# One-hot products of the dense tokens' weights: from float32 to bfloat16 pieces

## The reference, cut to what matters

```
idx = i_half * N_KEYS + i_half'            # 16 of 128 x 128 for each head
g = softmax(top_s)
h = gelu(einsum('td,thkd->thk', xb, u[idx]))
out = einsum('thk,thkd->td', g * h, v[idx])
```

## Time and profile before

| | us |
|---|---|
| median of three runs (1388.97 to 1390.58) | 1390.19 |
| the profiled execution's own time | 1392.18 |
| its span in the trace | 1390.4 |
| mean granted TensorE clock | 0.999 |

### The profile page before, as it was taken

One profiled execution on the slowest core, in us unless ns is written; L12 is line 12 of the kernel. 1 busy time (PEld: TensorE's weight loads), 2 busy tenths in 40 slices (PEclk: granted clock), 3 DMA queues, 4 the chain that ended last, 5 costly groups with the idle time before them and its releaser, 6 DMA issues.

```text
span 1390.4 us, 16195 instructions
## 1 busy us (share of the span) xinstructions
PE 1367.2 (98%) x5402; PEld 935.1 (67%) x5402; DVE 1056.4 (76%) x2365; ACT 438.4 (32%) x1219; POOL 599.5 (43%) x516
## 2 busy tenths in 40 slices
PE   7999999999999999999999999999999999999999
PEld 5656648567588888888899999995444444444443
DVE  4535445799899999998589899998768667766665
ACT  2533522444411111113677887882000000000000
POOL 0000001632855554442356655564667745544540
PEclk9999999999999999999999999999999999999999
DMA  8322334985999999996899999999999999999998
GB/s 308 138 108 111 121 125 183 362 314 196 403 389 411 409 352 374 342 350 234 299 377 407 385 398 395 389 382 402 388 410 409 410 409 409 409 409 409 410 409 311
DMA packets 121762, 467.68 MB, mean 336 GB/s; under 512 B 13776, under 2 KB 14160, under 8 KB 115152
## 3 DMA queue, kind: packets, MB, share of 16 engines
q0 software_dynamic: 73728, 268.47, 49.8%
q1 hardware_dynamic: 47664, 197.66, 36.8%
q10 hardware_dynamic: 288, 0.52, 0.1%
HBM read 462.67 MB, written 3.93 MB: 336 GB/s over the span
## 4 chain that ended last, share of the span: by engine, by line
PE 94%; DVE 3%; ACT 2%; issue 1%; DMA 0%; SPq 0%; ACTq 0%; DVEq 0%
PE BANKS L941 32%; PE BANKS L965 32%; PE BANKS L741 11%; PE BANKS L733 10%; PE BANKS L960 4%; PE BANKS L924 1%; PE BANKS L713 1%; PE BANKS L857 1%; PE BANKS L768 1%; PE BANKS L778 0%; DMA BIG<-w_in 0%; PE BANKS L829 0%; DVE NMX L1574 0%; ACT BIG L1122 0%; DVE UV L1638 0%
## 5 line engine op out<-in xcount | busy, mean ns | idle before, releaser
L1685 POOL DMA_INDIRECT UV<-u,IDX x152 | 174.1, 1145 | 398.8 <-DVE IDX L1513 261.2
L1685 POOL DMA_INDIRECT UV<-v,IDX x159 | 191.1, 1202 | 165.9 <-DVE UV L1638 91.3
L1643 DVE SCALAR_TENSOR_TENSOR X<-UV,HG,X 128x1024 f32<-128x1024 f32 x159 | 203.7, 1281 | 39.3 <-DMA UV<-v,IDX 37.1
L941 PE MATMUL BANKS<-T 128*128 128x256 f32 x1024 | 229.2, 379 | 0.0
L965 PE MATMUL BANKS<-T,BIG 128*128 128x512 f32 x512 | 225.2, 592 | 0.0
L965 PE MATMUL BANKS<-Y,BIG 128*128 128x512 f32 x512 | 225.1, 592 | 0.0
L941 PE MATMUL BANKS<-T,Y 128*128 128x256 f32 x992 | 221.9, 379 | 0.0
L1638 DVE SCALAR_TENSOR_TENSOR UV<-UV,Y 128x1024 f32<-128x1024 f32 x152 | 184.9, 1221 | 42.2 <-DMA UV<-u,IDX 40.8
L941 PEld LDWEIGHTS BANKS<-T 128*128 128x128 f32 x1024 | 192.0, 190 | 24.9 <-issue 0.2
L941 PEld LDWEIGHTS BANKS<-T,Y 128*128 128x128 f32 x992 | 186.0, 190 | 24.0
L965 PEld LDWEIGHTS BANKS<-Y,BIG 128*128 128x128 f32 x512 | 97.3, 190 | 122.5 <-issue 122.5
(11 more groups left out here) (258 smaller groups left out, 1222.2 us busy)
## 6 DMA issues: line engine op xcount, KB each, us to landing
T<-u_t SPq DMA_DIRECT2D x64, 512.0 KB
T<-v SPq DMA_DIRECT2D x64, 512.0 KB
Y<-v SPq DMA_DIRECT2D x64, 512.0 KB
Y<-u_t SPq DMA_DIRECT2D x62, 512.0 KB
BIG<-w_in SPq DMA_DIRECT2D x23, 1024.0 KB, 6.7
BIG<-w_q SPq DMA_DIRECT2D x16, 1024.0 KB, 7.4
BIG<-w_out SPq DMA_DIRECT2D x8, 1024.0 KB, 5.9
UV<-v,IDX POOLq DMA_INDIRECT x159
```

The source lines that it names most:

```text
L941: last = nc.tensor.matmul(PS[(i + 2) % 4][:, 0:HT], ub[:, c, :], T8[:, 1, c, :], start=(c == 0), stop=(c == KC - 1))
L1643: stt(xb, row, HG[:, n % 2, i % UNIT:i % UNIT + 1], xb, ALU.mult, ALU.add).then_inc(used, 1)
L1685: pool.indirect_dma_start(row_place(s), None, u if kind == "ru" else v, bass.IndirectOffsetOnAxis(IDX[:, b, c:c + 1], 0)).then_inc(row_in[ ...
```

## The change

The products of `og` are made in bfloat16. The one-hots are exact in it. The weight (float32, 24 bits of mantissa) is cut into three bfloat16 pieces of which the sum is the weight, so that each product becomes three that add up in PSUM: 12 products in a group in place of 4 float32 ones (which the trace counts as 8 MATMUL, two for each). A new step `sp` (`split_weights`) cuts the weights of a block, on DVE, straight from the PSUM bank of `sel`; the first two pieces lie in one 32-bit word (`WUPPER`), so that one scaled copy writes both. `oh` is now: DVE compares for j and for i, both in bfloat16, four tokens innermost; ACT scales the one-hot of j with `WUPPER` into `UPPER` (float32 words, read by PE as `HALVES`, every second bfloat16) and with `WLOWER` into `LOWER`. The bank is laid out token by token (t j) in place of (j t). ACT's part of `oh` waits for DVE's (`oh_j`), where before it waited for PE alone. `IOTAS`, a bfloat16 table of the key numbers, is written once. Small tables of the mixer (`DT`, `DTS` and others) become views of a new tile `STEPS`, which later holds the one-hot of j.

```diff
-    work += [first] + on("sel", 0) + rows(9) + on("oh", 0) + [second] + rows(3) + on("oh", 1) + [sums, keys, columns]
+    work += [first] + on("sel", 0) + rows(5) + on("sp", 0) + rows(4) + on("oh", 0) + [second] + rows(3) + on("oh", 1) + [sums, keys, columns]
...
+        if k == 2:
+            o += on("sp", 1)
...
+        KIJ = KT3[:, 0, :].bitcast(BF16).rearrange("p (a t) -> p a t", a=2)
+        WUPPER, WLOWER = KT3[:, 1, :], KT3[:, 2, :]
...
                 elif step == "og":
                     pe.wait_ge(oh_i, i + 1)
-                    pe.wait_ge(oh_ja, i + 1)
+                    pe.wait_ge(oh_w, i + 1)
                     if i in (0, 3):
-                        pe.wait_ge(selt_done, 4 if i else 2)
+                        pe.wait_ge(selt_done, 2 if i else 1)
+                        pe.wait_ge(split_done, 2 if i else 1)
...
-                    bank = PS[4 + i % 4][:, :].rearrange("p (j t) -> p j t", t=NTOK)
                     for k in range(NTOK):
-                        last = nc.tensor.matmul(bank[:, :, k], ONEHOT[:, i % 2, 0, k, :], ONEHOT[:, i % 2, 1, k, :],
-                                                start=True, stop=True)
+                        pieces = HALVES[:, i % 2, k, :, 1], HALVES[:, i % 2, k, :, 0], LOWER[:, i % 2, k, :]
+                        for m, piece in enumerate(pieces):
+                            last = nc.tensor.matmul(PS[4 + i % 4][:, k * P:(k + 1) * P], ONEHOT_I[:, i % 2, :, k], piece,
+                                                    start=(m == 0), stop=(m == 2))
...
                 elif step == "oh":
...
+                    act.wait_ge(oh_j, i + 1)
+                    for k in range(NTOK):
                         t = i * NTOK + k
-                        nc.scalar.activation(ONEHOT[:, i % 2, 1, k, :], IOTA, ACT.Abs, bias=KT3[:, 1, t:t + 1],
-                                             scale=-1.0).then_inc(oh_abs, 1)
...
+                        nc.scalar.activation(UPPER[:, i % 2, k, :], ONEHOT_J[:, i % 2, :, k], ACT.Copy,
+                                             scale=WUPPER[:, t:t + 1])
+                        last = nc.scalar.activation(LOWER[:, i % 2, k, :], ONEHOT_J[:, i % 2, :, k], ACT.Copy,
+                                                    scale=WLOWER[:, t:t + 1])
+                    last.then_inc(oh_w, 1)
...
+            def split_weights(i):
+                dve.wait_ge(selt_done, i + 1)
+                if i == 0:
+                    nc.vector.tensor_copy(IOTAS, bc(IOTA, 2, NTOK))
...
             def onehots(g):
...
+                tt(ONEHOT_J[:, g % 2, :, :], IOTAS, bc(KIJ[:, 1, part], 1, NKEY), ALU.is_equal).then_inc(oh_j, 1)
                 if g >= 2:
                     dve.wait_ge(gb_full, g - 1)
-                tt(ONEHOT[:, g % 2, 0, :, :], bc(IOTA, 1, NTOK), bc(KT3[:, 0, t0:t0 + NTOK], 2, NKEY),
-                   ALU.is_equal).then_inc(oh_i, 1)
+                tt(ONEHOT_I[:, g % 2, :, :], IOTAS, bc(KIJ[:, 0, part], 1, NKEY), ALU.is_equal).then_inc(oh_i, 1)
...
-                    tt(hb, hb, PS[4 + i % 4].rearrange("p (j t) -> p j t", t=NTOK)[:, 0:JS[i], :], ALU.mult)\
+                    tt(hb, hb, PS[4 + i % 4].rearrange("p (t j) -> p j t", t=NTOK)[:, 0:JS[i], :], ALU.mult)\
```

More of the change, by code:

```diff
@@ L314, in block_program @@
         SS = sb("SS", [P, 8 * NB])
[L315 to L321, removed]
+        STEPS = sb("STEPS", [P, 4 * NKEY])
+        ONEHOT_J = STEPS[:, :].bitcast(BF16).rearrange("p (q j t) -> p q j t", q=2, t=NTOK)
+        DTS = STEPS[:, 0:6 * NB * NH].rearrange("p (m n) -> p m n", m=6)
+        ACS = STEPS[:, 192:256].rearrange("p (b n) -> p b n", b=NB)
+        DT, DA, EACS, DTE, CD = (STEPS[:, 256 + 32 * m:288 + 32 * m].rearrange("p (b n) -> p b n", b=NB) for m in range(5))
         AH = sb("AH", [P, NH])
@@ L508, in q_at @@
             return hj if half else PH + hj % PH
-        def abs_count(g):
-            return sum(NTOK - ACT_FROM[i % 2] for i in range(g))
         def y_count(kind, b):
@@ L1520, in softmax_of @@
                 return tt(g3, g3, bc(SMALL[:, at:at + n], 2, TOPK), ALU.mult)
-            def onehots(g):
+            def split_weights(i):
+                dve.wait_ge(selt_done, i + 1)
+                if i == 0:
+                    nc.vector.tensor_copy(IOTAS, bc(IOTA, 2, NTOK))
+                part = slice(i * P, (i + 1) * P)
+                w, rest = PS[4 + 3 * i][:, 2 * P:3 * P], PS[4 + 3 * i][:, 3 * P:4 * P]
+                upper, lower = WUPPER[:, part], WLOWER[:, part]
+                ts(upper.bitcast(U32), w.bitcast(U32), HIGH, None, ALU.bitwise_and).then_inc(split_step, 1)
+                dve.wait_ge(split_step, 5 * i + 1)
+                tt(lower, w, upper, ALU.subtract).then_inc(split_step, 1)
+                dve.wait_ge(split_step, 5 * i + 2)
+                ts(rest.bitcast(U32), lower.bitcast(U32), HIGH, None, ALU.bitwise_and).then_inc(split_step, 1)
+                dve.wait_ge(split_step, 5 * i + 3)
+                tt(lower, lower, rest, ALU.subtract).then_inc(split_step, 1)
+                dve.wait_ge(split_step, 5 * i + 4)
+                ts(rest.bitcast(U32), rest.bitcast(U32), 16, None, ALU.logical_shift_right).then_inc(split_step, 1)
+                dve.wait_ge(split_step, 5 * i + 5)
+                tt(upper.bitcast(U32), upper.bitcast(U32), rest.bitcast(U32), ALU.bitwise_or).then_inc(split_done, 1)
+                dve.wait_ge(split_done, i + 1)
@@ L1523, in onehots @@
+            def onehots(g):
+                if g % (NGRP // HB) == 0:
+                    dve.wait_ge(selt_done, 2 if g else 1)
+                if g == 0:
+                    dve.wait_ge(x_away, 16)
+                if g >= 2:
+                    dve.wait_ge(oh_w, g - 1)
+                part = slice(g * NTOK, (g + 1) * NTOK)
+                tt(ONEHOT_J[:, g % 2, :, :], IOTAS, bc(KIJ[:, 1, part], 1, NKEY), ALU.is_equal).then_inc(oh_j, 1)
                 if g >= 2:
                     dve.wait_ge(gb_full, g - 1)
-                if g % (NGRP // HB) == 0:
-                    dve.wait_ge(selt_done, 4 if g else 2)
@@ L1654, in _ @@
                     onehots(i)
+                elif step == "sp":
+                    split_weights(i)
                 elif step == "gm":
```

41 lines of the change are left out of this document (16 added, 25 removed).

## The result

The changed kernel takes 1393.85 us in the median of 17 runs (1389.46 to 1398.32); the kernel before, timed beside it, 1390.34 (17 runs, 1388.22 to 1393.66). The ratio is 1.0024, interval 1.0013 to 1.0034: 1.8 to 4.7 us slower, 3.3 in the middle, where +0.9 was forecast. The profiled execution is one of the longest: 1397.83 us, span 1395.7. The spread is part of the finding.

A forecast was written before the change was run, and what follows sets the result against it. DVE and PE were taken to keep the same pace, DMA queues close behind. From 1390.19 us: first products −0.2, splits 0, one-hots +1.1, PE's other −10.4 not reaching the end: +0.9, 1391.0; range 1382 to 1405.

The forecast's parts named there:

- The likeliest case: Whole kernel: time within 0.2% of the kernel before, own range 1387.5 to 1393 us; chance 0.36.
- PE's products: og on PE: twelve bfloat16 records at 0.060 us replace eight float32 at 0.111, 0.72 us in place of 0.89.
- PE's saving as a whole: PE in the one-hot stage: 0.17 us less per group, 10.6 us of PE's own time.
- The saving does not reach the end: End of the one-hot stage: PE's other 10.4 us are not won, since DVE with its rows keeps the pace.
- `gm(62)` lets the v stage start: Start of the v stage: follows DVE's gm of group 62, ending at 947.29, first v product at 947.39.
- One-hots: DVE's comparisons: two bfloat16 at 0.35 us replace one float32 at 0.60; +5.6 us over 62 groups, +1.1 after cover.
- waits give back four fifths: DVE's row waits in the one-hot stage: shrink to absorb four fifths of the one-hots' +5.6 us, leaving +1.1.
- The split: DVE's weight split: six operations, 1.9 us; the first, about 2.6 with the CAST, hidden in idle time before oh(2); 0.
- The second split: DVE ahead of oh(4): about nothing, beside 3.2 us of waits; 1.9 us without them.
- ACT's slack: ACT's copies behind DVE's one-hot of j: og's operands ready at 784.7, PE there at 785.67, 1.0 us to spare.
- The end: Kernel's end: v stage unchanged at some 440 us; last row ends at 1382.52, ahead of the last instruction's 1387.24.
- The rival "faster": One-hot stage: DVE's row waits give way, pace falls to 4.21 to 4.28 us, −4 to −8.4 us; chance 0.30.

The follow-up runs named there:

- merged: Changed kernel with one DVE comparison of 1024 elements for i and j in place of two of 512; 1391.44 us, ratio 1.0006 to the kernel before.
- pe_packed: Kernel before with twelve bfloat16 products per og and the bank written token by token, DVE's one-hots as before, weights cut to bfloat16; 1392.16 us, ratio 1.0005.
- fewer_rows: Changed kernel with one more row in every eighth round of the one-hot stage, not every fourth; eight rows move to the v stage; 1391.29 us, ratio 1.0007.
- no_j_no_chain: Changed kernel without DVE's comparison for j from group 2 on, and with ACT not waiting for DVE; 1389.04 us, ratio 0.9987.
- no_j: Changed kernel without DVE's comparison for j from group 2 on, ACT still waiting for the comparison for i; 1390.53 us, ratio 1.0003.
- the second profile: Changed kernel run again unchanged for another profile; 1391.77 us in one run, span 1390.0.
- no_split: Changed kernel without DVE's six split operations and their wait, ACT copying the weights instead; 1392.30 us, ratio 1.0004.

## Why the forecast held, and where it was off

The time lies in the stated range, but that range reached from a gain of 8 us to a loss of 15. The likeliest case, no change within 0.2% (1387.5 to 1393), was missed by a little: 1.0024. The sum was right in its largest step, that PE's saving does not reach the end, and too low in what the change costs.

Two chains end the kernel together. Over the fourteen profiles the span ends no less than 3.77 us after the last v product starts (before, merged, pe_packed and others) and no less than 6.3 us after the last row ends (6.35 and 6.33 in the changed kernel, 6.31 in fewer_rows), and always at one of the two, to within 0.1 us. For the kernel before the chain of rows would have ended at 1382.5 + 6.3 = 1388.8 in one profile and 1389.4 in the other, where PE's ended at 1390.4 and 1389.8. So 0.4 to 1.6 us were all that a faster PE could win at the end, unless the rows came earlier too. In some profiles they did (1376.0 in pe_packed, 1379.1 in merged), in others they came later (1389.3), and of the medians only that of no_j_no_chain (0.9987) lies clear below the kernel before. What they would have to beat: from the start of the v stage on they are 206 rows and 128 tiles of `v` at 402 to 407 GB/s, and before it a round at PE's new pace would need 405, where the stage had 391.

- **PE's products**: 0.060 us forecast, 0.70/12 = 0.058 measured, in the new layout of the bank. The Trainium skill's 81 ns ("TensorE: Matmul & The Clock Gate", "Back-to-back issue gap") doesn't agree; the 0.111 of float32 against 0.058 does agree with its section "Weight-path perf modes — Fast Weight Load (FWL) and DoubleRow", by which other weights load about twice as fast. Whether the load or the 128 columns set the 0.058, no run separates. The layout is not what float32 paid for: before the change, sixteen float32 records into neighbouring words followed each other at (1.95 − 0.275)/15 = 0.112 us (a record's modelled length is 0.275), as `og`'s did at a stride:

```profile
91.80 1.95 PE L768 MATMUL BANKS<-BIG 128*128 128x128 f32 x16
```

- **PE's saving as a whole** was put at 0.17 us per group, 10.6 in all. `og` did become 0.19 shorter, but the `gl` behind it takes 3.51 from start to start in place of 3.45, so the pace went from 4.35 to 4.21: 0.14 per group, 9.0 in all.
- **The saving does not reach the end**: right. The reason was half right. Rows do hold DVE, and DVE holds PE. But the stage is not paced by "DVE's own work and what it waits", of which the first could be cut (no_j) with no gain in the stage; it is paced by the landing of rows. PE's idle time is near the forecast 0.17 per group (0.17 in the second profile, 0.28 in the first), but not spread evenly: most groups go at 4.21, and 13 or 19 intervals hold all of it. And the sentence that "`gm(62)` lets the v stage start" was wrong: 947.29 and 947.39 were neighbours by chance, and the changed kernel starts 2.2 us before that `gm` has ended.
- **One-hots**: 0.35 us each forecast; records of 418 and 444 ns, starts 0.34 apart, fit. That waits give back four fifths was the step least borne out: row waits were 0.38 per group in one profile (20.3 us over 240/4.49 groups) and 0.27 in the other, against 0.31 before.
- **The split**: the first was hidden as forecast; `oh(2)` had 2.93 us of idle time left, forecast 3. That number came by luck. The wait for ACT's copy did not stay at 4.32 when it moved; it became 8.00, as DVE comes to it four rows sooner. The 7 us from the copy to the first one-hots (637.63 to 644.65) are the split's 2.3 and the four rows' 4.7, not 4.32 + 2.6. The second split was put at nothing. It is a sum of 1.95 us of work and a wait of 2.19 for ACT's copy that the prediction left out; what it costs at the end isn't resolved (no_split). DVE at the first split, at the first one-hots, and at the second split:

```profile
637.63 0.43 DVE L1528 CAST KT<-CONST 128x512 bf16<-128x512 f32 x1 [8.00 <-ACT KT L1229]
...
644.65 0.41 DVE L1553 TENSOR_TENSOR STEPS<-KT 128x512 bf16<-128x512 bf16 x1
...
678.17 0.29 DVE L1532 TENSOR_SCALAR KT<-BANKS 128x128 uint32<-128x128 uint32 x1 [2.19 <-ACT KT L1229]
```

- **ACT's slack** of 1.0 us was about right for a group without a stall (0.8 and 0.9 on the mean from group 8 on) and wrong as cover: one late row took 1.49 us ahead of the stall at 784.44, and then `og` waits for ACT, ACT for DVE and DVE for the row.
- **The end**: the prediction saw the last row end at 1382.52, 4.7 us ahead of the last instruction, and left the rows out of the sum there; only its last sentence names them. With four additions and the store behind the last row the room was 0.4 to 1.6.

In the sum the mis-sized term is what remains of DVE's additions: +1.1 for the one-hots and 0 for the splits were forecast, and the whole measures +3.3 (1.8 to 4.7). How it divides stays open. By the ratios, taking away the chain, the second comparison or the split each gives 2.8 to 3.5 us back, the chain and the second comparison together 5.1. These don't add up, only the chain's interval and that of both together lie clear of the changed kernel's, and rows of one kernel end up to 6 us apart between executions for a reason that no run shows. Two more things weren't tried: a kernel with fewer rows in all, which would show PE's 9 us at the end, and a ring of more than five buffers, which would tell the queues' rate from the time that a row takes to land.

The rival "faster" looked in the right place, the bytes of a round. In the changed kernel it fails in the stage: tiles that are asked for earlier did not raise the rate toward 405 (378 and 391 GB/s in the two profiles), and the pace was 4.49 and 4.38 on the mean. In fewer_rows the pace of 4.21 comes, and the gain fails at the end, where the rows that were put off come due.

## What to carry to other kernels

Before costing a faster engine, follow every chain that reaches the end, with what stands behind its last step, and take the smallest distance as the most that can be won; here it was about 1 us against the 9 that PE saved. Where a cut in one engine's work turns into waits of the same length, look for a supply (here bytes per round against the queues' best rate), and try a smaller demand rather than less work. When an operand's type changes, cost the layout of the output with it.

## What the runs showed of the hardware

- Twelve bfloat16 products of 128 columns into a PSUM bank at a stride of four words took 1.27 us, into neighbouring words 0.69 to 0.70: 0.106 against 0.058 each. Float32 records of 128 columns took 0.111 at that stride (`og` before the change) and 0.112 into neighbouring words (L768).
- DVE's read of PSUM at a stride of 128 words in `gm` took no longer than in a row: 554 against 555 ns on the mean, and over the 62 shapes that both kernels have 1 ns less.
- A row fetch for 64 of 128 tokens was hardly cheaper: 106 of them took 55.4% of the DMA engines' time between 700 and 940 us, where 124 whole ones took 69.3%. The queues ran at a busy share of 1.03 while they moved 219 GB/s, and a tile of `u` landed after 10.2 us, 6.6 in the changed kernel's second profile.
